# Hybrid decoder trunk on eight cores: mixer chunks cut into parts and interleaved, DMA issues held to the FFN's progress, mixer weights cast at first use

## The reference

```python
for l in range(DEPTH):                                   # DEPTH = 2
    h = rms_norm(x, ffn1_norm[l])
    x = x + 0.5 * swiglu(h, ffn1_w1[l], ffn1_w3[l], ffn1_w2[l])     # D_FF = 2816
    h = rms_norm(x, mix_norm[l])
    x = x + token_mixing(h, ...)                         # u = h @ w_in, four head groups
    h = rms_norm(x, ffn2_norm[l])
    x = x + 0.5 * swiglu(h, ffn2_w1[l], ffn2_w3[l], ffn2_w2[l])
# token_mixing: A  native sparse attention: compressed, selected (top 8 blocks of 64) and
#                  sliding-window (512) branches, gated
#               B  short gated convolution, C  grouped sliding-window attention (128) with sinks
#               D  causal pooling of windows 2, 4, 8, 16 minus the token
#               then an RMS norm by group and @ w_out
```

## Time and profile before

| | |
|---|---|
| Median of 3 runs | 6281.04 us (6272.51 to 6290.34) |
| The profiled execution | 6294.04 us, its span 6292.6 us (slowest of 8 cores, 6197.2 to 6292.6) |
| PE | 4966.1 us busy, 79% |
| DVE | 3292.4 us, 52% |
| ACT | 2458.1 us, 39% |
| POOL | 1478.9 us, 24% |
| DMA | 1146.47 MB, 182 GB/s in the mean |
| Chain that ended last | PE 45%, DMA 20%, DVE 13%, issue 9% |

### The profile page before, as it was taken

The page is one execution under the profiler, slowest core; times in us unless marked ns, Lnnn a source line. Parts: engine busy times, 40 slices in busy tenths (PEclk is TensorE's granted clock), DMA queues, the critical chain, the costliest instruction groups (busy, mean ns, idle before and its releaser), DMA issues.

```text
span 6292.6 us, 92670 instructions; the slowest of 8 cores (6197.2 to 6292.6 us)
## 1 busy us (share of the span) xinstructions
PE 4966.1 (79%) x27469; PEld 2243.0 (36%) x27469; DVE 3292.4 (52%) x6766; ACT 2458.1 (39%) x4661; POOL 1478.9 (24%) x1713
## 2 busy tenths in 40 slices
PE   1567888788877887778888788888887788788588
PEld 0223334343333443234343343333343334344233
DVE  2455555555546556455554646454455655555243
ACT  1113445353624453135362434425253345353421
POOL 3112222122213322112222222212122223222111
PEclk9788999999988999889999999998998999999677
DMA  9876566647576657764636565564667765646235
GB/s 147 193 215 197 177 224 194 201 145 228 148 220 165 204 176 217 191 195 148 218 130 212 168 196 163 188 194 152 210 171 201 197 202 166 216 130 220 70 127 172
DMA packets 421832, 1146.47 MB, mean 182 GB/s; under 512 B 48288, under 2 KB 48672, under 8 KB 420416
## 3 DMA queue, kind: packets, MB, share of 16 engines
q1 hardware_dynamic: 401456, 1055.51, 51.2%
q0 software_dynamic: 19888, 85.02, 9.6%
HBM read 936.47 MB, written 304.14 MB: 197 GB/s over the span
## 4 chain that ended last, share of the span: by engine, by line
PE 45%; DMA 20%; DVE 13%; issue 9%; ACT 5%; POOL 4%; another core or an unknown queue 1%; SPq 1%; DVEq 1%; ACTq 0%; POOLq 0%
PE ps L550 44%; DMA W<-w 4%; DMA XM<-xd 3%; DMA XP<-xd 3%; DMA xd<-XP 3%; POOL RQK L566 2%; DMA xd<-XM 2%; ACT ETP L559 2%; DVE XP L568 1%; DVE GP L566 1%; DVE W L566 1%; DMA XF<-xd 1%; DVE SMP L566 1%; DMA XF<-xT 1%
## 5 line engine op out<-in xcount | busy, mean ns | idle before, releaser
L550 PE MATMUL ps<-XO,W 128*128 128x512 f16 x9856 | 2422.6, 394 | 310.7 <-DVE W L566 87.4
L550 PE MATMUL ps<-GP,W 128*128 128x512 f16 x4928 | 1292.8, 411 | 295.9 <-DVE XP L568 149.0
L550 PEld LDWEIGHTS ps<-XO,W 128*128 128x128 f16 x9856 | 938.9, 100 | 1482.8 <-issue 643.8
L566 POOL TENSOR_TENSOR GP<-GP 128x512 f16<-128x512 f16 x576 | 673.1, 1179 | 998.2 <-DVE GP L566 966.9
L568 DVE SCALAR_TENSOR_TENSOR XP<-ps,XP 128x512 f32<-128x512 f32 x768 | 519.4, 688 | 626.7 <-DMA XP<-xd 366.4
L550 PEld LDWEIGHTS ps<-GP,W 128*128 128x128 f16 x4928 | 481.0, 103 | 933.9 <-issue 555.5
L559 ACT ACTIVATE ETP<-ps,RQK 128x512 bf16<-128x512 f32 (+1 forms) x1072 | 656.3, 637 | 310.5 <-PE ps L550 295.6
L550 PE MATMUL ps<-MX,WM 128*128 128x512 f16 x2944 | 730.6, 401 | 46.4 <-DVE MX L568 24.0
L558 ACT COPY ps<-ps 128x512 f32<-128x512 f32 x608 | 348.4, 573 | 927.6 <-PE ps L550 607.6
L559 ACT ACTIVATE FT<-ps 128x512 f16<-128x512 f32 x704 | 417.8, 596 | 676.3 <-PE ps L550 668.6
L568 DVE SCALAR_TENSOR_TENSOR FT<-FT,ps 128x512 f16<-128x512 f16 x704 | 481.1, 683 | 381.2 <-ACT FT L559 376.3
(11 more groups left out here) (156 smaller groups left out, 3872.0 us busy)
## 6 DMA issues: line engine op xcount, KB each, us to landing
W<-s SPq DMA_DIRECT2D x264, 896.0 KB, 5.7
xd<-XP SPq DMA_DIRECT2D x448, 256.0 KB, 4.2
XP<-xd SPq DMA_DIRECT2D x448, 256.0 KB, 4.4
s<-W SPq DMA_DIRECT2D x88, 896.0 KB, 5.8
XM<-xd SPq DMA_DIRECT2D x256, 256.0 KB, 4.7
WM<-swin SPq DMA_DIRECT2D x240, 256.0 KB, 4.3
XF<-xd SPq DMA_DIRECT2D x192, 256.0 KB, 4.0
W<-w POOLq DMA_DIRECT2D x88, 512.0 KB, 7.8
```

Source lines behind the costliest of these rows:

```text
L550: inst = e.matmul(out, lhsT=lhsT, rhs=rhs, start=st, stop=sp_, skip_group_check=True)
L566: return e.tensor_tensor(**a)
```

## The change

**Planner's numbers.** Assumed durations are replaced throughout: a PE time factor `PEF` of 1.04, pow of RQK 0.8 to 8.02 us, exponentials 0.6 to 0.686, and so on; a DMA issue on SP 0.1 to 0.33; latencies between engines and DMA rate and latency as below. A dependency on the own engine counts 0.1 (none on PE).

**Gate.** `cur` is the due place of the last FFN matmul planned. A DMA whose `pos` is past `cur`, and any other operation past `cur` + 0.5, is held in `gate` until the FFN comes there, or until nothing else is left. Allocation of several tiles for one operation becomes all or nothing.

**Mixers.** `mixer_chunk` becomes a generator cut by `yield` into parts. `mixer_stream` advances the four chunks of a sequence and layer in one list: between the parts of a chunk's blocks stand the last parts of the chunk before and the first of the chunk after. Parts are recorded among half steps by weight, and `mixer_pos` spreads the due places of a whole stream over its interval (same four intervals) by PE time and half the ACT time. The query broadcasts move behind projections and compression. KW gets a third block of 512 (12 instead of 8 keys' blocks).

**Loads.** `init_mixer_w` goes. Chunk 0 of sequence 0 loads each mixer weight through GpSimd's queue with a cast and stores it; others load it as before. XF goes and XP has 6 pages (was 3 + 3), XM 3 (was 2), FR 2 (was 1). `prep_ffn` and `stats_from_x` return parts, run ahead of the four parts of the second and the first W2 phase, with loads due 25 matmuls early. In the first part of a W2 phase a product's last matmul is recorded apart. Two PM tiles become `opp`. The scratch for GpSimd's DMA descriptors is halved to 4096.

The diff, cut to its core:

```diff
 NDSEM = 96
 EPOCH = 2000
-LAT = 0.20
-LATPE = 0.30
-DMARATE = 300e3
-DMALAT = 2.2
+LAT = 0.17
+LATPE = 0.25
+LATSELF = 0.10
+PEF = 1.04
+DMARATE = 290e3
+DMALAT = 3.0
 
 
...
+        n = len(self.ops)
+        ops = self.ops
+
+        def ready(o, t):
+            if (o.kb and o.pos > cur) or o.pos > cur + 0.5:
+                hpush(gate, (o.pos, t, o.i))
+            else:
+                hpush(fut[o.eng], (t, o.pos, o.i))
...
+                ps, t, i = hpop(gate)
+                cur = ps
+                hpush(fut[ops[i].eng], (max(t, max(free.values())), ps, i))
+                continue
             if best is None:
                 for p in self.pools:
...
+            if e == "pe" and o.ffn and o.pos > cur:
+                cur = o.pos
+                while gate and gate[0][0] <= cur:
+                    ps, tg, i = hpop(gate)
+                    hpush(fut[ops[i].eng], (max(tg, t), ps, i))
...
-                    hpush(fut[q.eng], (max(es, t), q.pos, q.i))
+                    ready(q, max(es, t))
         self.order = order
...
-        XF = pool("XF", 3, 512, F32)
-        XP = pool("XP", 3, 512, F32)
+        XP = pool("XP", 6, 512, F32)
+        XM = pool("XM", 3, 512, F32)
...
-                        xt = XF.tile()
-                        xload(xt, s, tc, k)
+                        xt = XP.tile()
+                        xload(xt, s, tc, k, pos=G.pos - 25 / 924)
                         xap = (lambda xt=xt: xt.ap())
...
         def prep_ffn(s, l, fi, hf, tiles=None):
...
+            def part(j):
+                if j == 0:
+                    for n, tc in ((1, n1), (2, n2)):
+                        rss[n] = bcast_rs(RST[(s, tc)], FRP, PM, FR, opp=True)
+                B = {}
+                for n, tc in ((1, n1), (2, n2)):
+                    for hk in (1, 2):
+                        kc = j + 4 * (hk - 1)
+                        if tiles is None:
+                            xt = XP.tile()
+                            xload(xt, s, tc, kc, pos=G.pos - 25 / 924)
+                            xap = (lambda xt=xt: xt.ap())
...
+                o = tsums(B, 1, XO, "dve", 0.42)
+                for k in ops:
+                    ops[k] += o[k]
+            return ops, part
...
                 for j in range(4):
+                    setpos()
+                    for f in side[j::4] if not last else side[j:j + 1]:
+                        f()
                     one(j)
...
             g1 = w13_group(0)
-            w2_group(0, g1, False)
+            w2_group(0, g1, False, early() if early is not None else [])
             g2 = w13_group(1)
-            setpos(-20)
-            nxt = prep_next() if prep_next is not None else None
-            w2_group(1, g2, True)
+            nxt, part = prep_next()
+            w2_group(1, g2, True, [lambda j=j: part(j) for j in range(4)] if part is not None else [])
             return nxt
 
-        def init_mixer_w(l):
-            G.pos = 0.55 if l == 0 else 5.0
-            for i in range(15):
-                dma(swin[l, i], winr[l, i], 256, [], [("swin", l, i)], eng="pool")
-            for i in range(2):
-                dma(swtm[l, i], wtmr[l, i], 268, [], [("swtm", l, i)], eng="pool")
-            for i in range(4):
-                dma(scw1[l, i], cw1r[l, i], 256, [], [("scw1", l, i)], eng="pool")
-            for i in range(8):
-                dma(swout[l, i], woutr[l, i], 256, [], [("swout", l, i)], eng="pool")
...
-            def wload(src, key, width=1024):
+            def wload(src, orig, key, width=1024):
                 t = WM.tile()
-                dma(lambda: t.ap(0, width), src, width * 0.25, [key], [t])
+                if s == 0 and c == 0:
+                    dma(lambda: t.ap(0, width), orig, width * 0.375, [], [t], eng="pool")
+                    dma(src, lambda: t.ap(0, width), width * 0.25, [t], [key])
+                else:
+                    dma(lambda: t.ap(0, width), src, width * 0.25, [key], [t])
                 return t
...
-            pl("tt", 0.8, [rqk, "NHALF"], [rqk], out=rq, in0=rq, in1=NHALF[:, 0:48], op=ALU.pow)
...
+            pl("tt", 8.02, [rqk, "NHALF"], [rqk], out=rq, in0=rq, in1=NHALF[:, 0:48], op=ALU.pow)
+
+            yield
             pb = proj(3)
             kv2 = []
...
+            cqt = []
+            for qi in range(4):
...
+
+            for kk in (0, 1, 4, 5):
+                yraw[kk] = MX.tile()
+            yield
+            extra = ((lambda: None, lambda: None, lambda: None, lambda: None), (lambda: do_b(0), lambda: do_d(0), lambda: do_b(1), lambda: do_d(1)),
+                     (lambda: gn_fm(((2, 3), (6, 7))), lambda: None, lambda: None, lambda: None), (lambda: None, lambda: None, lambda: None, lambda: None))
             for b4 in range(4):
-                block(b4)
-                extra[b4]()
-            gn_fm(((2, 3), (6, 7)))
+                n_ = 0
+                for _ in block(b4):
+                    extra[b4][n_]()
+                    n_ += 1
...
+        def mixer_stream(s, l, w0, w1):
+            gens = [mixer_chunk(s, l, c) for c in range(4)]
+            items = []
+
+            def adv(c, w):
+                items.append((w, gens[c]))
+            for w in (5, 12, 4, 5, 3):
+                adv(0, w)
+            for c in range(4):
+                adv(c, 2)
+                nb = lambda b4: (1.5, 4.0, 1.0 * (4 * c + b4 + 1), 5.0)
+                for b4 in range(4):
+                    side = {0: [(c - 1, 5)] * 4 if c else [], 2: [(c + 1, 4), (c + 1, 12)] if c < 3 else [],
+                            3: [(c + 1, 4), (c + 1, 5), (c + 1, 3)] if c < 3 else []}.get(b4, [])
+                    for k in range(4):
+                        if k < len(side):
+                            adv(*side[k])
+                        adv(c, nb(b4)[k] + (5 if b4 == 1 else 0))
+            for k in range(4):
+                adv(3, 5)
+            tot = float(sum(w for w, _ in items))
+            cum = 0.0
+            out = []
+            for w, g in items:
+                cum += w
+                out.append((w0 + (w1 - w0) * cum / tot, g))
+            return out
...
-        chunks = []
-        for s, l, a, b in ((0, 0, 1.0, 4.2), (1, 0, 4.2, 7.8), (0, 1, 7.8, 11.2), (1, 1, 11.2, 14.4)):
-            for c in range(4):
-                chunks.append((s, l, c, a + (b - a) * c / 4, a + (b - a) * (c + 1) / 4))
-
-        ev = [(k + 0.8, 0, k) for k in range(16)] + [(ch[4], 1, i) for i, ch in enumerate(chunks)]
-        ev.sort()
+        ev = [(k + 0.8, 0, k, None) for k in range(16)]
+        mixers = []
+        for i, (s, l, a, b) in enumerate(((0, 0, 1.0, 4.2), (1, 0, 4.2, 7.8), (0, 1, 7.8, 11.2), (1, 1, 11.2, 14.4))):
+            mixers.append(([], a, b))
+            ev += [(key, 1 + i, j, g) for j, (key, g) in enumerate(mixer_stream(s, l, a, b))]
+        ev.sort(key=lambda v: v[:3])
...
```

More of the change, by code:

```diff
@@ L227, in schedule @@
                     best = e
+            if best is None and gate:
+                ps, t, i = hpop(gate)
+                cur = ps
+                hpush(fut[ops[i].eng], (max(t, max(free.values())), ps, i))
+                continue
             if best is None:
@@ L243, in schedule @@
                     pl = tl.pool
-                    if pl.head != tl.idx and not tl.opp:
-                        park.setdefault(id(tl), []).append(o)
-                        blocked = True
-                        break
+                    if not tl.opp:
+                        ahead = sum(1 for x, _ in got if x.pool is pl and not x.opp)
+                        if pl.head + ahead != tl.idx:
+                            park.setdefault(id(tl), []).append(o)
+                            blocked = True
+                            break
                     bs, ba = None, 1e17
+                    used = [x for x in got if x[0].pool is pl]
                     for s in range(pl.np - tl.n + 1):
                         a = max(pl.avail[s:s + tl.n]) if tl.n > 1 else pl.avail[s]
-                        if a < ba:
+                        if a < ba and not any(s < y + x.n and y < s + tl.n for x, y in used):
                             ba = a
@@ L261, in schedule @@
                         break
+                    got.append((tl, bs))
+            if not blocked:
+                for tl, bs in got:
+                    pl = tl.pool
                     tl.slot = bs
@@ L267, in schedule @@
                     tl.prev = prev
[L268 to L271 removed]
+                    if not tl.opp:
+                        pl.head += 1
+                        if pl.head < len(pl.tiles):
+                            for q in park.pop(id(pl.tiles[pl.head]), ()):
+                                hpush(fut[q.eng], (t, q.pos, q.i))
             if blocked:
@@ L491, in build_program @@
         FQ = pool("FQ", 2, 512, BF16)
[L492 removed]
+        FR = pool("FR", 2, 512, F16)
         FRP = pool("FRP", 1, 512, F16)
@@ L667, in stats_from_x, with part @@
             acc = STT.tile()
```

(56 more changed lines are left out.)

299 lines of the change are left out of this document (147 added, 152 removed).

## The result

The changed kernel took 5261.1 and 5299.7 us, the kernel before 6272.5 to 6295.4: a ratio of 0.840 (95% interval 0.834 to 0.846), or some 5281 us for the 6286 of before. All times in this document are of executions in which neither die ran at a lower clock than the other (two of the changed kernel's four).

The account below looks back on a forecast made before the run. Latency and order, not arithmetic, were taken to bound the kernel. Terms -130 - 90 - 90 - 135 - 120 - 95 + 50 = -610 took 6294.0 to 5684, and the runs' median, 13 lower, gave 5670 us; range 5300 to 6250.

Parts of the forecast that it names:

- Start: First 200 us: casting weights at first use and gating DMAs fills PE earlier, -130 us; bounds 0 and -148.
- Pow: Query norms on GpSimd in the middle: planning 8.02 us and moving broadcasts cuts PE's MRP wait, -90; bounds 0 and -122.
- Pages: FFN residual pages in W2 phases: a pool of 6 removes half of 173.7 us, -90; bounds +120 and -174.
- The other waits of the middle: 703 us of many small waits in the middle: a fifth goes, -135 us.
- Clock: Middle: with less idle time, part of 483 us of low clock and unfilled pipelines goes, -120; bounds 0 and -161.
- End: 5840 to 5990 us, last chunk alone without FFN matmuls: shares by weight close the hole, -95; bounds 0 and -150.
- rival (e): The gate doesn't pull late work forward, so the hole at the end stays; counted as part of (b).
- Added costs: Chunk 0's cast loads and stores +25, shared XP queue and shorter load leads +25; bounds together 0 and +230.
- rival (d): The gate starves norm, statistics and residual loads, making the kernel slower: 6625 us; chance 0.12.
- Rival (a): Middle packs deeper, half to two thirds of the way to its best density: 5467 to 5271, say 5400 us; chance 0.22.
- (b): Waits change hands: only start, pow and half the end are won, 6065 us; chance 0.15.
- (c): The lower clock spreads: a denser middle runs at 0.81 for half its FFN matmuls, 6020 us; chance 0.06.

Follow-up runs that it names:

- kernel 1: The kernel before plus only the gate and mixer weights cast at first use; old durations, whole chunks, 3 pages each for XP and XF: 6007 us.
- kernel 11: The kernel before plus new durations, one pool of six pages and mixer weights cast at first use; no gate, old streams: 6014.3 us, ratio 0.962.
- kernel 4: The changed kernel planned with the old durations, latencies and DMA rate: 5507.2 us.
- kernel 9: The kernel before planned with the new durations, latencies and DMA rate, nothing else: 6167.0 us, ratio 0.987.
- kernel 6: The changed kernel with only the pow of RQK planned at the old 0.8 us instead of 8.02: 5348.6 us, ratio 0.860.
- kernel 2: The changed kernel with the pages back at XP 3 and XF 3 instead of one pool of 6: 5525.5 us.
- kernel 10: The kernel before plus new durations and one pool of six pages: 6068.6 us, ratio 0.971.
- kernel 12: The changed kernel without gate and interleaving of chunks, and with norm work in one piece: 5270.6 us, ratio 0.844.
- kernel 8: The kernel before with one pool of six pages in place of XF and XP: 6050 us, ratio 0.968.
- kernel 3: The changed kernel without interleaving, each stream's chunks recorded whole, one after the other: 5292.9 us.
- kernel 5: The changed kernel without the gate: 5194.0 us, ratio 0.832.
- kernel 7: The changed kernel with all norm work of the next half step in one piece ahead of the second W2 phase: 5254.2 us, ratio 0.842.

## Why the prediction was right in sign and too cautious

- **Start, -130: measured -145** (131 by the count of FFN matmuls). Right, bounds included. FFN matmuls run in the first 100 us (184 on XO from 50 to 100), and the casts of the earlier trace rows are gone. Kernel 1 and kernel 11 both have this full start: it is the casts, not the gate as well.
- **Pow, -90: measured -117** (122.1 to at most 5.6 us of MRP). Right in the wait. Place and duration each remove most of it (kernels 4 and 9). The step missed the pow's second victim: masks queued behind it on GpSimd (99.5 us of ETP in kernel 6), which is why its duration is worth 67 us even where hardly anybody waits for MRP.
- **Pages, -90: measured -68** by the waits of the middle (120.1 to 52.2), well inside the bounds. But undoing the pages costs 244, and doing them alone gains 200. The price of an edit was read from the line of one wait, and in kernel 2 that line is 55 of the 211 us of idle time that the edit makes; the other waits grow with it.
- **The other waits of the middle, -135: measured -346** (703 to 415 - 6 - 52 = 357). This is the step that failed, the mis-sized term: a fifth was chosen, half went. It was chosen with the argument that in-order queues keep their waits because DMA landings vary. They do vary (page loads still land after 5.9 us at the median), yet the waits went. What the runs show in its place: these waits belong to the same edits that were priced by one line each. Undoing the pages alone brings back 211 us of PE's idle time, 55 on the line for XP; undoing the durations alone brings back 197, 60 on the lines for MRP and ETP. How the two share the 346 with the new recording was not separated. Behind it stood a missing question: who sets the pace of the middle, FFN or mixers? The waits of the earlier trace rows don't answer it, since a slow FFN and slow mixers in step look like many small waits. Kernels 9 to 12 answer it: with the mixers as they were recorded and placed before, a faster FFN ends in stretches of its own standing.
- **Clock, -120: measured -147** for clock and fill on core 1, with 530 us less idle instead of 315. That is 147 / 530 = 0.28 us per idle us, where the forecast had 0.51. But 454 us of core 1's middle ran at 0.81. On core 6 it is 483 - 261 = 222 over 945 - 423 = 522, or 0.43. So the direction and nearly the rate were right, more idle time went than the bound allowed for, and the clock of 0.81, which the sum left out, took a part back.
- **End, -95: measured -94** (150 less the 56 of moved work). But the reason given, shares by weight, wasn't needed: kernel 1 closes the hole with equal quarters, the gate and the casts, and kernel 11, with the casts and no gate, doesn't. The rival (e) said the gate couldn't do this; that was wrong.
- **Last half step, not forecast: -78.** It ran at clock 0.77 for 302 us, and runs at 0.99 for 225. At the prices of the earlier trace rows its about 930 matmuls should take some 200, so the stretch was priced nowhere, though it lay open. Some 30 us of it are not the change's at all: only cores 4 and 5 of the kernel before had 0.81 there (283 and 287 us for the last 924 FFN matmuls, the others 250 to 260). Most of the rest is the pages': 249 to 261 us in kernel 2, 227 to 228 on the cores of kernel 8 without 0.81.
- **Added costs, +50:** not to be seen. VectorE's waits for loads into XP are 51.0 + 77.8 (norm) + 33.6 + 15.0 (from xT) = 177 us; the mark for rival (d) was 1000. So (d) is out, though the gate does cost some 50 us beside right durations.
- **Rivals.** Rival (a), packing at half to two thirds, was 5467 to 5271 with 5400 named; its deeper end came true, and the range should have gone below it: the text itself gave 1178 us as the bound and then cut at 5300. (b) is out by the middle's idle time, 415 us for 945. (c) is out by the middle's clock of 0.95; its lower clock is there, on core 1 for 576 of 5299 us, not for half of the FFN's matmuls.
- **The marks.** All five came true: FFN matmuls in the first 100 us, MRP 5.6, XP 77.0 over the whole span, the middle 91% busy at 0.95, no stretch without FFN matmuls.

In sum: the terms with a row of their own (start, pow, pages, end) came to -424 for the -405 forecast. The 384 us missed are, to 1 us, those 19, the waits without a row (211), the last half step (78, of which some 30 are luck of the cores compared), costs that didn't come (50) and clock (27).

## What to carry to other kernels

Where two streams of work meet at dependencies, ask first which of them sets the pace: a gain in the other comes back as a stretch in which it stands, and the stretches without its instructions, sliced evenly over the span, show it at once. The same edit was worth 226, 84 and about 0 us, depending on what else was slow, so an edit undone in the final kernel and the same edit done alone give two different answers, and neither holds elsewhere. The line of one wait can be a quarter of what its cause costs. A wrong number in a planner also costs through what is queued behind the instruction (59 us of masks in kernel 6), where a list of who waits for its result shows 2. And before small differences between kernels are read, compare cores that had the same clock.

## What the hardware showed

The clock of 0.81 of the earlier trace rows is in the changed kernel too, in stretches of its dense middle. One of them, on core 1 and then on core 2 of the same die:

```profile
1100.00:1150.00 50.00, 50.00 (x271) 22.48 (x270) 22.88 (x43) 28.50 (x53) 22.93 (x22) 0.81 0.31 104
...
1100.00:1150.00 50.00, 49.91 (x357) 26.70 (x355) 28.51 (x61) 34.76 (x74) 25.78 (x28) 1.00 0.43 143
```

In these 50 us all eight cores have PE busy for 49.6 us or more; cores 0 and 1 are at 0.81, the six others at 1.00. So density alone doesn't call for it, nor does it take a whole die.

The traces' clock records show that it takes neighbours together. In the changed kernel cores 0 and 1 have it from 1074 to 1233 us, 2 and 3 from 4916 to about 5075, 4 and 5 from 2450 to 2611, 6 and 7 from 3387 to 3549 (each counted from the core's own start). In the kernel before it is cores 4 and 5 near the end, and 6 and 7 between 114 and 630 us; so in the earlier trace rows core 5 has it and 6 doesn't. Here are the times at 0.81 in profiled executions, and the spans:

| Kernel | us at 0.81, cores 0 to 7 | spans of the cores | median, 0.18 us off for each us at 0.81 |
|---|---|---|---|
| before | 0, 0, 0, 0, 290, 314, 373, 363 | 6197 to 6293 | 6201 |
| changed | 593, 576, 285, 282, 157, 161, 158, 158 | 5223 to 5299 | 5204 |
| 2 | 124, 128, then 0 | 5482 to 5524 | 5505 |
| 3 | 0 on all | 5240 to 5276 | 5264 |
| 4 | 0 on all | 5467 to 5507 | 5477 |
| 5 | 146 and 153 on 4 and 5 | 5149 to 5184 | 5158 |
| 6 | 147, 154 on 2 and 3, 142, 125 on 6 and 7 | 5300 to 5348 | 5307 |
| 7 | 267 and 264 on 6 and 7 | 5199 to 5266 | 5218 |
| 12 | 0 on all | 5230 to 5270 | 5251 |

The 0.18 is an estimate from the changed kernel: cores 1 and 6 are 75 us apart in span with 576 and 158 us at 0.81, and 15 us apart in idle time. So rival (c) had the mechanism and not its spread: it costs core 1 some 100 us. What the change wins on the clock is time at half speed: the cores of the kernel before spend 946 to 1040 us of the span at 0.5, those of the changed kernel 310 to 385. What picks the cores for 0.81, and when, stays open; no kernel was made for it.
